# The first expert unit's rows by one-hot products from SBUF, gathers from the second unit on

## The reference

```
gsel = argmax(glog)                      # one of 4 groups
tv, ti = top_k(elog[group], 2)           # two of its 8 experts
tw = softmax(tv) * gw
act = silu(x @ w_gate[e]) * (x @ w_up[e]) * combine[..., e]
y  += act @ w_down[e]                    # over 32 experts, 1024 -> 256 -> 1024
x   = x + g2 * y
```

## Time and profile before

| what | value |
|---|---|
| median of 3 runs | 1538.37 us (1536.35 to 1540.29) |
| profiled execution | 1534.32 us |
| its span | 1532.3 us |
| mean granted TensorE clock | 0.943 |
| busy: VectorE, ScalarE, GpSimd | 524.9, 338.9, 116.5 us |

### The profile page before, as it was taken

How to read it: one execution, slowest core, us unless ns; L and a number is a source line. 1 busy time by engine, 2 the same in 40 slices (tenths; PEclk the granted TensorE clock), 3 DMA queues, 4 the chain that set the end, 5 groups by cost and what they waited for, 6 DMA issues and landing times.

```text
span 1532.3 us, 16990 instructions
## 1 busy us (share of the span) xinstructions
PE 1325.9 (87%) x6462; PEld 807.7 (53%) x6462; DVE 524.9 (34%) x1078; ACT 338.9 (22%) x722; POOL 116.5 (8%) x140
## 2 busy tenths in 40 slices
PE   6999788999988997786999997978878989977874
PEld 3545585466973333332466547978767733332322
DVE  3010663323242111011557906677762421110114
ACT  2100314233221111110326213121232211111111
POOL 2400000000001111110000001000000011111100
PEclk9999888999998999999999998999988989999998
DMA  9942477165456999994623200100016469999943
GB/s 357 347 153 98 179 191 265 33 258 205 192 204 227 392 418 418 418 418 180 204 86 134 69 14 0 29 1 1 1 75 242 188 231 404 415 417 418 418 184 124
DMA packets 81301, 329.79 MB, mean 215 GB/s; under 512 B 18791, under 2 KB 19985, under 8 KB 56512
## 3 DMA queue, kind: packets, MB, share of 16 engines
q1 hardware_dynamic: 66224, 300.54, 50.5%
q0 software_dynamic: 14992, 28.10, 5.6%
HBM read 321.09 MB, written 30.58 MB: 230 GB/s over the span
## 4 chain that ended last, share of the span: by engine, by line
PE 58%; DMA 18%; DVE 14%; issue 6%; ACT 2%; SPq 1%; POOL 0%; DVEq 0%; ACTq 0%; POOLq 0%
PE psum L912 19%; PE psum L1244 12%; PE psum L1006 9%; DMA ring<-in_moe_w_up 6%; DMA arena<-in_moe_w_up 5%; PE psum L1270 3%; DMA wide<-in_moe_w_up 3%; PE psum L938 3%; PE psum L1001 2%; DMA arena<-in_ada_w 2%; DVE arena L2325 1%; PE psum L881 1%; DVE wide L2285 1%; DMA arena<-h_rows,slot_token 1%; PE psum L945 1%
## 5 line engine op out<-in xcount | busy, mean ns | idle before, releaser
L912 PE MATMUL psum<-wide,ring 128*128 128x384 f32 x704 | 237.4, 497 | 4.2 <-ACT wide L1542 1.9
L912 PEld LDWEIGHTS psum<-wide,ring 128*128 128x128 f32 x704 | 164.3, 237 | 69.3 <-issue 6.3
L1244 PE MATMUL psum<-arena 128*64 128x512 f32 x480 | 152.6, 627 | 29.7 <-DMA ring<-in_moe_w_up 14.2
L1244 PE MATMUL psum<-ring,arena 128*64 128x512 f32 x384 | 138.0, 637 | 14.5 <-DMA wide<-in_moe_w_up 7.4
L1006 PE MATMUL psum<-ring 128*128 128x128 f32 x872 | 114.0, 289 | 17.6 <-issue 8.3
L2198 DVE TENSOR_TENSOR arena<-arena,psum 128x256 f32<-128x256 f32 x34 | 14.3, 421 | 309.0 <-ACT arena L1685 309.0
L1006 PEld LDWEIGHTS psum<-ring 128*128 128x128 f32 x872 | 108.0, 201 | 22.9 <-issue 13.0
L912 PE MATMUL psum<-ring,wide 128*128 128x512 f32 (+2 forms) x336 | 116.1, 507 | 0.0
L1244 PEld LDWEIGHTS psum<-arena 128*64 128x64 f32 x480 | 47.9, 144 | 108.4 <-issue 105.6
L881 PE MATMUL psum<-cst 128*128 128x128 f32 (+1 forms) x304 | 88.3, 442 | 10.0 <-issue 7.2
L1244 PE MATMUL psum<-wide,arena 128*64 128x512 f32 x224 | 86.2, 601 | 5.4 <-DMA arena<-in_moe_w_up 5.4
(11 more groups left out here) (496 smaller groups left out, 1683.2 us busy)
## 6 DMA issues: line engine op xcount, KB each, us to landing
ring<-in_ada_w SPq DMA_DIRECT2D x23, 2048.0 KB, 13.0
arena<-in_moe_w_gate SPq DMA_DIRECT2D x28, 1024.0 KB, 13.9
arena<-in_moe_w_up SPq DMA_DIRECT2D x28, 1024.0 KB, 20.3
arena<-in_moe_w_down SPq DMA_DIRECT2D x28, 1024.0 KB, 20.5
ring<-in_moe_w_gate SPq DMA_DIRECT2D x24, 1024.0 KB, 13.2
ring<-in_moe_w_up SPq DMA_DIRECT2D x24, 1024.0 KB, 19.0
ring<-in_moe_w_down SPq DMA_DIRECT2D x24, 1024.0 KB, 21.2
ring<-in_w_in_odd SPq DMA_DIRECT2D x7, 2048.0 KB, 8.1
```

What stands on the lines that cost most here:

```text
L912: ins = mm(out, lhs(k), rhs(k), start=(k == 0), stop=(k == n - 1))
L1244: ins = mm(psum[half, 2 + s, :].rearrange("p (w f) -> p w f", w=2), hg[s][:, k, half], buffers[UNITS[q][h] % BUFFERS][0][:, :, k, :], star ...
```

## The change

A new pair of jobs, "h0" 0 and 1, stands between "rk" and "ix". VectorE takes, as soon as the ranks are there, the ranks of experts 0 and 16 (each 16th column of comb times order) and compares them with 1 to 64: this gives hot_first, for each token tile 128 one-hot columns, one for each slot of unit 0. TensorE multiplies each 128-column piece of hrows by them, summed over three token tiles: 24 products, whose results are unit 0's rows, turned already. ScalarE copies the two banks to hg[0]. So turn(0), its copy and gather(0) are gone, Pool begins with gathers 1 and 2, and the counts that the semaphores are compared with are shifted (loads, turns). The fillers ahead of "ix" and of turn(0) are gone. TensorE clears one bank (that with number 2) before gate_up(0) and the others behind it. SyncE waits for the second "h0" before it loads into `wide`. VectorE's wait for the ranks moves up.

```diff
-        ... [("ct", l), ("rk", l), ("ix", l)] +\
+        ... [("ct", l), ("rk", l), ("h0", l, 0), ("h0", l, 1), ("ix", l)] +\
...
+            return PAIRS // 2 * l + (n + 1) // 2          # loads(l, n)
+        def turns(l, n):
+            return (PAIRS - 1) * l + n
...
+        hot_first = yrow[1][:, 0:TILES * P].rearrange("p (c s) -> p c s", c=TILES)
...
                 sp.wait_ge(S("h_rows_out"), 16 * TILES * (l + 1))
+                sp.wait_ge(*computed("h0", l, 1))
                 sp.wait_ge(S("expert_ids"), 2 * l + 1)
...
-                    gather(0)
                     gather(1)
+                    gather(2)
                     for n in range(PAIRS):
-                        if n + 2 < PAIRS:
-                            pool.wait_ge(S("gathered_turned"), PAIRS * l + n + 1)
+                        if n and n + 2 < PAIRS:
+                            pool.wait_ge(S("gathered_turned"), turns(l, n))
                             gather(n + 2)
                         scatter(n)
...
+            def first_rows(l):
+                for half in range(2):
+                    b = issue("h0", l, half)
+                    pe.wait_ge(S("h_rows"), TILES * (l + 1))
+                    pe.wait_ge(S("hot_rows"), (2 * TILES + 1) * l + 1)
+                    for k in range(4):
+                        for c in range(TILES):
+                            ins = mm(b[:, tok(k)], hrows[:, c, tok(4 * half + k)], hot_first[:, c, :],
+                                     start=(c == 0), stop=(c == TILES - 1))
+                    ready(ins)
...
                 b = issue("ix", l)
-                keep_busy(b, 3)
...
-                clear_banks()
-                keep_busy(psum[:, 7, :], 5)
-                turn(0)
+                clear_banks((2,))
                 for q in range(PAIRS):
                     gate_up(q)
+                    if q == 0:
+                        clear_banks((0, 1, 3, 4, 5, 6))
...
-                copy_turned(0)
+                for half in range(2):
+                    act.wait_ge(*computed("h0", l, half))
+                    take(fn(hg[0]...[:, half], bank("h0", l, half), ACT.Copy), "h0", l, half)
...
+                dve.wait_ge(*computed("rk", l))
+                o_(tt(place_first, comb[:, :, 0::HALF], order[:, :, 0::HALF], ALU.mult))
+                tt(hot_first..., iota[:, 1:CAP + 1]..., bc(place_first, 3, each), ALU.is_equal)\
+                   .then_inc(S("hot_rows"), 1)
                 dve.wait_ge(*computed("ct", l))
...
-                dve.wait_ge(*computed("rk", l))
```

More of the change, by code:

```diff
@@ L202, in experts @@
     def experts(l):
-        return [("hr", l, c, half) for c in range(TILES) for half in range(2)] + [("ct", l), ("rk", l), ("ix", l)] +\
+        return [("hr", l, c, half) for c in range(TILES) for half in range(2)] + [("ct", l), ("rk", l), ("h0", l, 0), ("h0", l, 1), ("ix", l)] +\
             [("yt", l, m) for m in range(KD)]
@@ L1212, in rows_out, with clear_banks @@
                         ready(ins)
[L1214 removed]
+            def clear_banks(which):
                 for n in range(at[0] - BANKS, at[0]):
[L1217 removed]
+                    if n % BANKS in which:
+                        pe.wait_ge(free[n % BANKS], n // BANKS + 1)
             def gathered(l):
[L1220 to L1221 removed]
                 kind = "gathered_"
@@ L1226, in turn @@
                     pe.wait_ge(S(f"{kind}hrow{q % 2}_in"), 16 * loads(l, q))
-                    if q:
-                        pe.wait_ge(S(f"{kind}hg"), PAIRS * l + q)
+                    if q > 1:
+                        pe.wait_ge(S(f"{kind}hg"), turns(l, q - 1))
                     for k in range(KD):
@@ L1235, in gate_up @@
                     s = q % 2
-                    pe.wait_ge(S(f"{kind}hg"), PAIRS * l + q + 1)
+                    if q:
+                        pe.wait_ge(S(f"{kind}hg"), turns(l, q))
+                    else:
+                        pe.wait_ge(*taken("h0", l, 1))
                     for n in sorted(set(UNITS[q])):
@@ L1673, in copy_turned @@
                 def copy_turned(q):
-                    act.wait_ge(S(f"{kind}turned"), PAIRS * l + q + 1)
+                    act.wait_ge(S(f"{kind}turned"), turns(l, q))
                     if q >= 2:
@@ L1678, in copy_turned @@
                         .then_inc(S(f"{kind}hg"), 1)
-                copy_turned(0)
+                for half in range(2):
+                    act.wait_ge(*computed("h0", l, half))
+                    take(fn(hg[0].rearrange("p (w k) s -> p w (k s)", w=2)[:, half], bank("h0", l, half), ACT.Copy), "h0", l, half)
                 for q in range(PAIRS):
@@ L2133, in router @@
                 counts = bank("ct", l)[:, 0:EXPERTS]
+                order = bank("rk", l)[:, 0:TILES * EXPERTS].rearrange("p (c e) -> p c e", c=TILES)
+                dve.wait_ge(*computed("rk", l))
+                place_first = slots_f[:, 4].rearrange("p w c -> p (w c)").rearrange("p (c e) -> p c e", c=TILES)
+                o_(tt(place_first, comb[:, :, 0::HALF], order[:, :, 0::HALF], ALU.mult))
+                each = [P, TILES, 2, CAP]
+                tt(hot_first.rearrange("p c (e s) -> p c e s", e=2), iota[:, 1:CAP + 1].unsqueeze(1).unsqueeze(1).to_broadcast(each),
+                   bc(place_first, 3, each), ALU.is_equal).then_inc(S("hot_rows"), 1)
                 dve.wait_ge(*computed("ct", l))
@@ L2150, in router @@
                 o_(tt(at_home[:, HALF - 1::HALF], hole, hole_sum, ALU.subtract))
-                dve.wait_ge(*computed("rk", l))
-                order = bank("rk", l)[:, 0:TILES * EXPERTS].rearrange("p (c e) -> p c e", c=TILES)
                 where = R[11][:, :, 0:EXPERTS]
```

4 lines of the change are left out of this document (2 added, 2 removed).

## The result

The changed kernel takes 1529.97 us (median of 8 runs, 1523.79 to 1532.41), the kernel before 1539.36 (8 runs, 1536.35 to 1543.21): a ratio of 0.9934, 95% interval 0.9914 to 0.9954, 9.4 us less. The forecast was 1521.2, 17.2 less, with a range that ended at 1529: the sign was right, and the gain a bit over half of what was forecast. A second series gave 1531.80 (12 runs), ratio 0.9953 [0.9932, 0.9975]. Two slow executions in a later series (1775.54 and 1651.20 us, with granted clocks of 0.73 and 0.81) count in no interval. The profiled execution took 1528.15 (span 1526.1, mean granted clock 0.935), against 1534.32.

A forecast was written before the change was run, and what follows sets the result against it. The prediction took the first gather, which everything waits for, as the bound: 9.8 us gained at turn(1) less 1.2 of clock is 8.6 a layer, 17.2 for both, so 1538.37 - 17.2 = 1521.2 us, range 1513 to 1529.

The forecast's parts named there:

- the mechanism and its place: Expert stage's head: everything waits for the first gather; without it gate_up(0) starts 12.4 us earlier, new wait before turn(1).
- The landing: Gather 1 before turn(1): lands at 473.2, taken between 472.8 (same delay as before) and 473.6 (drained queue).
- its reading of a drained queue: Gather 1 lands when the queue is drained of expert 4's 3 MB, at 473.6 as before.
- the two signs of being wrong: turn(1) gains under 5 us, or new waits for weights appear before unit 8.
- VectorE's 0.8 us: Two new VectorE operations after the rank products, the second 0.56 us, make everything behind, slot lists above all, 0.8 later.
- The lists: Slot-list products end 0.3 us behind the last hot row; slot_token at 463.5 instead of 464.26, 0.8 earlier.
- Rival 1: Low clock at the new products' start: they end at 464.2, gain 12 to 14 in all, 1525 us; chance 0.19.
- The worst case: New one-hot products with 24 records at half clock in 5.6 us and 24 in 2.8, ending at 464.2.
- SyncE: Added wait ahead of expert 4's load: cost 0 with 0.7 us of cover, since products end at 461.3, issue is 463.07.
- The clock after the new wait: Slow TensorE clock behind the wait before turn(1): 1.2 us lost per layer, bounds 0 and 3.0.
- The second rival: Gather 1 slips in among the 3 MB, landing by 471; 12.0 to 12.4 gained per layer, 1514 us; chance 0.08.
- The sum: Per layer 9.8 gained at turn(1) less 1.2 of clock is 8.6, both layers 17.2: 1521.2 us.

The follow-up runs named there:

- hold_gate_up: Changed kernel with gate_up(0) made to wait until gather 1 has landed; 1546.66 us, ratio 1.0044 to the kernel before.
- lists_ahead: Changed kernel with VectorE's writes of slot_token, share and slot_row moved ahead of the six instructions forming expert_id; 1528.12 us, ratio 0.9929.
- fill_turn: Changed kernel with three filler products between gate_up(0) and turn(1); 1522.83 us, ratio 0.9912 to the kernel before.
- load_behind: Changed kernel with SyncE's load into `wide` held until VectorE has written `flag`, so it queues just behind gather 1; 1529.17 us, ratio 0.9921.
- before_gather_first: Kernel before, with SyncE's load into `wide` and all behind it held until gather 0 has landed; 1536.44 us, ratio 0.9966.

## Why the prediction was right or wrong

**Right: the mechanism and its place.** The first gather was the link that all waited for; gate_up(0) covers it now (`hold_gate_up` takes the whole gain away). gate_up(0) starts at 11.1 us after the ranks instead of 22.5, 11.4 earlier (forecast 12.4). The new wait stands where it was said to, before turn(1), with the gather as its releaser: 2.95 us in layer 0 (forecast 2.6). The landing takes 8.7 us (forecast 8.7), with 8.3 to 9.4 in the eight stages; the forecast took a value between two mechanisms, so the close hit is partly luck. (In layer 0 some 2.9 MB of weights had moved by the landing, which is near its reading of a drained queue.) The gain is handed on to the last unit (6.8 of 6.7), and neither of the two signs of being wrong appeared.

**Right by its rows: VectorE's 0.8 us.** The hot rows begin 0.83 us later, counted from the ranks (460.68 in the changed kernel, whose ranks start at 452.11, against 461.01 in the earlier trace rows). VectorE's operation of 384 elements took 0.56.

**Wrong: "The lists".** This is the step that failed. It put slot_token "at 463.5 instead of 464.26, 0.8 earlier"; it came 0.5 later (11.5 against 11.0 after the ranks), 1.2 a layer off. Three things were not in it.
- *VectorE's own order, 0.5 us.* The forecast let slot_token follow the last hot row by 0.4 us. VectorE has six instructions between them and needs 1.2. Before, they cost nothing: the lists were 0.8 us later still. With faster lists they are the floor, 11.06 to 11.13 in five of the eight stages, which is the old time less 0.8 for the lists plus 0.8 for the new operations. `lists_ahead` moves them and gets 10.56. It was a question that the old timeline could have answered: what stands in the same engine's list once this wait is shorter?
- *The lists at full rate, 0.35 us.* They were to end 0.3 us behind the last hot row. In `lists_ahead`, with the products and the lists wholly at full rate, they end 0.68 behind it: the first starts 0.15 after the first hot row and the twelve records take 1.51 us.
- *The low clock in the products, 0.4 us.* Rival 1, in part: the low stretch stands at their start, as it says, but is shorter in most stages. The products ended at 9.6 on average, not at 8.0, and in three stages slot_token came at 11.5, 12.2 and 12.6. (In two of these the write also came 0.46 us behind the last list record, not 0.11 as elsewhere; why is not shown.) The worst case was well sized (10.9 for the end of the products, measured at most 10.9); that the stages would fall between the cases was missed.

**Wrong too: "SyncE", cost 0 with 0.7 us of cover.** The load into `wide` goes out 11.0 us after the ranks on average instead of 9.5, since the wait for the products is now the longer one. In SyncE's waits of the changed kernel, layer 0:

```profile
SPq L690 <- PE psum L1209: 8.7, 1, 8.7
```

**turn(1)** therefore gains 8.2 us a layer, not 9.8.

**The clock after the new wait** costs 1.5 us a layer, 1.2 was taken: within its bounds of 0 and 3.0, and `fill_turn` shows that it is the clock. "TensorE: Matmul & The Clock Gate" of the Trainium skill, section HAM oscillation, warns of work with transfer waits between; the traces agree in seven of eight stages, and as far as the products up to the first down go, not a whole unit (down in 5.35 us against 3.65, the next gate_up back at 6.87).

**The second rival** was right in what it said of idle queues (4.1 us) and wrong for this order of issue: 0.4 to 2.3 us behind the first of the 3 MB, the gather takes 8.3 to 9.4. "DMA: Bandwidth & Descriptors", section Queues, rings and completion order, of the Trainium skill, has each DMA engine take turns between its queues. The queues of the changed kernel agree with that from 469.00 on, when both move; before, for 4.4 us after the gather's issue, only the weights' packets move. What holds the gather's first packet that long is not shown.

**The sum.** Forecast 8.6 a layer, measured 6.8 at the last gate_up: 1.6 less at turn(1), 0.3 more of clock. That makes 13.6 for both layers where 17.2 was forecast. The measured difference is 9.4 in the first series and 7.9 in the second. Of the 4 us that are still missing in the first, some 1.3 lie between the last gate_up and the output transposes: counted to these, the stages are 8.1 and 4.2 us shorter on average, 12.3 in all. The rest is not in the stages. The untouched stretch between them is 3.3 us longer on average in the profiles with the products (485.0 against 481.7), with 478.9 to 487.6 found with them and 477.6 to 488.0 without. Renumbering is not seen to make it. Whether it is a small systematic effect on the phase in which the clock falls or only chance can't be told from eight and twelve profiles; this is left open. The prediction's scale of 0.3% for what can be told apart was right, its range of 1513 to 1529 too narrow: its ends were built from terms of the stages alone, and nothing was put for a stretch that moves by 10 us from one execution to the next.

**Better than both.** All variants with fillers or the move lie between 1522.8 and 1528.1. `fill_turn`, 0.9912 [0.9883, 0.9942], is clearly faster than the kernel before; that it beats the changed kernel is seen in the stage (1.9 us at gate_up(1), 1.7 at the last gate_up), while the intervals of the whole times overlap.

## What to carry to other kernels

When a wait is shortened, read the waiting engine's own list between the last input and the waiting instruction: what used to lie inside the wait is the new floor. Where one transfer stands ahead of everything, give it work to hide behind first, then look at what is queued in front of it; moving a weight load from about 1.5 us ahead of the gather to 1.2 us behind it was worth 4 us of landing here, and held back until the landing the same load cost more than it gave. And before the gain of a small change is read off two profiles, compare a stretch that the change does not touch.

## What the hardware showed that was not expected

- The same 2289 records between the two expert stages took 477.5 to 488.0 us in executions of one kernel, with a granted clock of 0.95 and 0.93: with the same work, a 1.5 ms kernel moves by 10 us with the clock.
- A gather of up to 128 rows of 4 KB from DRAM (the first two move 0.52 MB together in `load_behind`) lands in 4.1 to 4.5 us if it is issued 1.1 to 1.3 us ahead of 3 MB of weights, and in 8.3 to 9.4 if it is issued 0.4 to 2.3 us behind them: its first packet then moves 4.2 to 4.5 us after the issue and not 1.7. The weight loads lose less: the three of expert 4 landed in 5.1, 7.4 and 10.2 us in the changed kernel and in 5.7, 8.7 and 10.8 in `load_behind`.
- Filler products meant to hold the clock ran for the most part at half of it themselves when they came after a pause (7.27 us for ten records in `before_gather_first`, as in the earlier trace rows, where the earlier trace rows has eight in 3.60), and then lasted longer than the wait that they cover.
